# A two-block transformer kernel: order of work in the attention pairs and the convolution branch of the first block

## The reference

```
proj = u @ w_in                       # q, k, v, conv input a | g, gates g_attn | g_conv
attn = softmax(q k^T / 8, causal) v   # 8 heads of 64 (one key block of 256: plain causal attention)
h    = a * sigmoid(g)
h    = depthwise_conv(h, 31 taps) + b # 512 channels
h    = silu(layer_norm(h))
y    = (sigmoid(g_attn) * (attn @ w_attn_br) + sigmoid(g_conv) * (h @ w_conv_pw)) @ w_out
x    = layer_norm(alpha * x + (1 + gt1) * y)
x    = layer_norm(alpha * x + (1 + gt2) * (relu(u2 @ w_up)^2 @ w_down))
```

## Time and profile before

| what | value |
|---|---|
| median of 3 runs | 1812.81 us (1811.41 to 1814.45) |
| span of the profiled execution | 1813.6 us (no other time of it is given) |
| PE busy | 1755.5 us, 97% |
| DVE busy | 1275.5 us, 70% |
| ACT busy | 891.5 us, 49% |
| DMA | 346.29 MB, mean 191 GB/s |
| mean granted TensorE clock | 0.997 |

### The profile page before, as it was taken

The page is one execution under the profiler, slowest core; times in us unless marked ns, Lnnn a source line. Parts: engine busy times, 40 slices in busy tenths (PEclk is TensorE's granted clock), DMA queues, the critical chain, the costliest instruction groups (busy, mean ns, idle before and its releaser), DMA issues.

```text
span 1813.6 us, 26735 instructions
## 1 busy us (share of the span) xinstructions
PE 1755.5 (97%) x9254; PEld 1450.9 (80%) x9254; DVE 1275.5 (70%) x1973; ACT 891.5 (49%) x1530; POOL 57.3 (3%) x111
## 2 busy tenths in 40 slices
PE   8999999998999999998999999999999999999998
PEld 3776778996766779987998977788889989778886
DVE  5788887667788885568557987655555588865555
ACT  1456434443455444444556664544455667544443
POOL 0000010000000000002000000000000000000000
PEclk9999999999999999999999999999999999999999
DMA  8866568774866566663665444555646645345553
GB/s 300 267 213 218 162 216 301 253 230 133 264 220 209 185 210 209 209 190 110 210 215 156 131 142 141 174 185 184 190 153 200 215 131 160 117 155 182 184 186 126
DMA packets 216040, 346.29 MB, mean 191 GB/s; under 512 B 19611, under 2 KB 113353, under 8 KB 215673
## 3 DMA queue, kind: packets, MB, share of 16 engines
q1 hardware_dynamic: 213448, 338.89, 58.3%
q0 software_dynamic: 1632, 5.39, 1.0%
q10 hardware_dynamic: 850, 0.54, 0.1%
HBM read 343.69 MB, written 1.07 MB: 190 GB/s over the span
## 4 chain that ended last, share of the span: by engine, by line
issue 79%; PE 12%; DVE 4%; DVEq 1%; POOLq 1%; POOL 1%; ACT 0%; DMA 0%; SPq 0%; ACTq 0%
PE acc L150 2%; PE acc L148 2%; PE acc L149 2%; PE prod L223 1%; PE prod L225 1%; PE prod L224 1%; DVE w_lo L134 1%; DVEq L937 1%; PE prod L148 1%; DVE proj L938 1%; PE prod L150 1%; PE prod L149 1%; PE turn L262 0%; DVE x_res L938 0%; DVE x_res L936 0%
## 5 line engine op out<-in xcount | busy, mean ns | idle before, releaser
L134 DVE TENSOR_TENSOR w_lo<-w_raw,w_hi 128x1024 fp32r<-128x1024 f32 (+2 forms) x584 | 643.7, 1122 | 308.6 <-ACT w_hi L128 302.9
L128 ACT CAST w_hi<-w_raw 128x1024 fp32r<-128x1024 f32 (+2 forms) x584 | 557.9, 968 | 406.6 <-PE acc L150 186.3
L148 PE MATMUL prod<-w_hi,hT_hi 128*128 128x512 f32 (+2 forms) x880 | 319.8, 363 | 4.7 <-ACT proj_b L1949 3.6
L150 PE MATMUL prod<-w_hi,hT_lo 128*128 128x512 f32 (+2 forms) x880 | 313.0, 356 | 0.0
L149 PE MATMUL prod<-w_lo,hT_hi 128*128 128x512 f32 (+2 forms) x880 | 312.3, 355 | 0.0
L148 PEld LDWEIGHTS prod<-w_hi,hT_hi 128*128 128x128 f32 x880 | 166.3, 189 | 25.0 <-DVE gates L2202 5.9
L150 PEld LDWEIGHTS prod<-w_hi,hT_lo 128*128 128x128 f32 x880 | 166.3, 189 | 15.4
L149 PEld LDWEIGHTS prod<-w_lo,hT_hi 128*128 128x128 f32 x880 | 166.8, 189 | 14.6
L223 PE MATMUL prod<-uT_hi,w_hi 128*128 128x256 f32 x448 | 127.1, 284 | 1.6 <-DVE w_lo L134 1.1
L148 PE MATMUL prod<-w_hi,uT_hi 128*128 128x512 f32 x304 | 124.6, 410 | 2.7 <-DVE uT_lo L301 1.3
L224 PE MATMUL prod<-uT_lo,w_hi 128*128 128x256 f32 x448 | 126.4, 282 | 0.0
(11 more groups left out here) (349 smaller groups left out, 2836.6 us busy)
## 6 DMA issues: line engine op xcount, KB each, us to landing
w_raw<-in_w_in_dram SPq DMA_DIRECT2D x72, 512.0 KB, 3.8
ada_raw<-in_w_ada_dram SPq DMA_DIRECT2D x68, 512.0 KB, 6.7
w_raw<-in_w_in_dram SPq DMA_DIRECT2D x192, 172.0 KB, 2.4
w_raw<-in_w_up_dram SPq DMA_DIRECT2D x64, 512.0 KB, 4.4
w_raw<-in_w_down_dram SPq DMA_DIRECT2D x64, 512.0 KB, 4.5
w_raw<-in_w_gate_dram SPq DMA_DIRECT2D x128, 192.0 KB, 2.6
w_raw<-in_w_ffn_gate_dram SPq DMA_DIRECT2D x88, 256.0 KB, 3.6
w_raw<-in_w_ffn_up_dram SPq DMA_DIRECT2D x88, 256.0 KB, 4.3
```

Source lines behind the costliest of these rows:

```text
L128: act.copy(self.hi[:, s, 0:cols], self.raw[:, s, 0:cols]).then_inc(self.hi_done, 1)
L134: dve.tensor_tensor(self.lo[:, s, 0:cols], self.raw[:, s, 0:cols], self.hi[:, s, 0:cols].bitcast(F32), ALU.subtract).then_inc(self.lo_done, 1)
L148: pe.matmul(out, a_hi, w_hi, start=first and c == 0, stop=False)
L150: mm = pe.matmul(out, a_lo, w_hi, start=False, stop=last and c == chunks - 1)
```

## The change

On DVE the minima of the scores, in every pair, stand directly behind the gating, ahead of `steps(counts[1])`, and these steps follow behind the inverses together with `counts[2]`. On ACT, in the last pair alone, the order behind `split_hi(nxt + 2)` becomes: copies of the turned probabilities, tanh of the gate tile, partial sums, high part of the attention rows, copy of the modulation sum, `split_hi(nxt + 3)`, `conv_take`. On TensorE the last `mod_sum` moves from behind group `at + 1` to directly behind `pair_end(3)`, ahead of the wait for the attention rows' low part. Behind the pairs ACT makes two weight halves ahead of the tanh of the convolution's rows instead of three behind them, and two behind the takes of the convolution's rows instead of one. DVE makes one low half ahead of its takes of these rows instead of two. No instruction is added or left out.

```
@@ ACT, pair(t) @@
                     W.split_hi(act, nxt + 2)
-                    take_tile(nt, this + 3, [...], ACT.Tanh, 0.5)
-                    W.split_hi(act, nxt + 3)
+                    gate_take = lambda: take_tile(nt, this + 3, [...], ACT.Tanh, 0.5)
+                    if t < PAIRS - 1:
+                        gate_take()
+                        W.split_hi(act, nxt + 3)
                     for h in range(2):
                         H.take(act, n, h)
+                    if t == PAIRS - 1:
+                        gate_take()
                     part_take(2 + t)
                     H.out_hi_part(act, n, ...)
+                    if t == PAIRS - 1:
+                        ada_take(layer(l, 2 + t, SUMS), chunk(mod2, NT), acc[1:2])
+                        W.split_hi(act, nxt + 3)
                     conv_take(t, layer(l, F_TAPS[t], F_ALL))
                     if t < PAIRS - 2:
                         hpad_take(t + 2, l)
-                    ada_take(layer(l, 2 + t, SUMS), chunk(mod2, NT), acc[1:2])
+                    if t < PAIRS - 1:
+                        ada_take(layer(l, 2 + t, SUMS), chunk(mod2, NT), acc[1:2])
 
                 for t in range(PAIRS):
                     pair(t)
+                split(layer(l, G_IN + G_HALF, G1), 2)
                 for tok in range(TOKS):
                     act.wait_ge(conv_y, layer(l, tok, TOKS).count(1))
                     act.activation(conv_sig[:, tok, :], conv_tok[:, tok, :], ACT.Tanh, scale=0.5).then_inc(conv_tanh, 1)
-                split(layer(l, G_IN + G_HALF, G1), 3)
                 for n in range(2):
                     T.take_hi(act, layer(l, F_CONV + n, F_ALL), cT[0][:, :, n * P:(n + 1) * P], scale=0.5,
                               view=lambda s: s.rearrange("p (c t) -> p c t", c=4))
-                split(layer(l, G_IN + G_HALF + 3, G1), 1)
+                split(layer(l, G_IN + G_HALF + 2, G1), 2)
@@ DVE, pair(t) @@
                     if t < PAIRS - 2:
                         gated(t + 2)
-                    steps(counts[1])
                     for h in range(2):
                         H.lows(dve, n, h, None, None)
                     W.split_lo(dve, nxt + 1)
                     for h in range(2):
                         H.inverse(dve, n, h)
-                    steps(counts[2])
+                    steps(counts[1] + counts[2])
@@ DVE, behind the pairs, j is the half of the branch's columns @@
                     W.split_lo(dve, layer(l, at + 4 + 2 * j, G1))
-                    W.split_lo(dve, layer(l, at + 5 + 2 * j, G1))
+                    if j == 1:
+                        W.split_lo(dve, layer(l, at + 5 + 2 * j, G1))
                     if j == 0:
                         for n in range(2):
                             place = lambda p: p[:, :, n * P:(n + 1) * P]
                             T.take_lo(dve, layer(l, F_CONV + n, F_ALL), ...)
+                        W.split_lo(dve, layer(l, at + 5 + 2 * j, G1))
@@ TensorE @@
                 pair_end(PAIRS - 1)
+                mod_sum(1 + PAIRS, acc[1])
                 pe.wait_ge(H.out_done, layer(l, PAIRS - 1, PAIRS).count(2))
                 at = G_IN
                 W.multiply(pe, layer(l, at, G1), aT, 0, NT, KG, outs, True, False, vacant=...)
                 conv_turn(PAIRS - 1)
                 W.multiply(pe, layer(l, at + 1, G1), aT, 2, NT, KG, outs, False, True)
-                mod_sum(1 + PAIRS, acc[1])
```

More of the change, by code:

```diff
@@ L837, in pair @@
                     W.split_hi(act, nxt + 2)
-                    take_tile(nt, this + 3, [chunk(proj[:, tok, :], NT, GA0) for tok in range(TOKS)], ACT.Tanh, 0.5)
-                    W.split_hi(act, nxt + 3)
+                    gate_take = lambda: take_tile(nt, this + 3, [chunk(proj[:, tok, :], NT, GA0) for tok in range(TOKS)],
+                                                  ACT.Tanh, 0.5)
+                    if t < PAIRS - 1:
+                        gate_take()
+                        W.split_hi(act, nxt + 3)
                     for h in range(2):
                         H.take(act, n, h)
+                    if t == PAIRS - 1:
+                        gate_take()
                     part_take(2 + t)
                     H.out_hi_part(act, n, aT[0][:, t, :] if last else aT[0][:, bass.ds(t, 1), :].rearrange("p a s -> p (a s)"))
+                    if t == PAIRS - 1:
+                        ada_take(layer(l, 2 + t, SUMS), chunk(mod2, NT), acc[1:2])
+                        W.split_hi(act, nxt + 3)
                     conv_take(t, layer(l, F_TAPS[t], F_ALL))
```

## The result

| | before | after |
|---|---|---|
| median | 1812.48 us (4 runs, 1811.41 to 1814.45) | 1804.01 us (4 runs, 1800.67 to 1806.32) |
| ratio, 95% interval | | 0.9949 (0.9936 to 0.9962) |
| span of the profiled execution | 1813.6 us | 1798.9 us |
| from the end of pair 0's scores to the convolution branch's product, layer 0 | 84.82 us | 80.38 us |
| the same, layer 1 | 83.77 us | 80.28 us |

A forecast was written before the change was run, and what follows sets the result against it. TensorE, busy 97%, was taken as the bound, with time only in its gaps or slow-clock stretches. Layer 0's 1.98 + 0.73 and layer 1's 1.07 + 0.73 made 4.5 us: median 1808.3 us, range 1806.5 to 1811.3.

The forecast's parts named there:

- The lead as pair 3 begins: Pairs 1 and 2: transposes freed of waits for scaled probabilities, gaining 0.85 + 0.22 = 1.07 us.
- the first reading of the prediction: TensorE, whole program: waits for scaled probabilities cost 2.5 us in four places, the size of what the change can reach.
- Pair 3: Last pair: transposes gain another 0.56 us; the value product starts directly behind the modulation rows, at 178.65 instead of 181.46.
- The next bound: Convolution's turn: fourth w_hi holds DVE 1.4 us, TensorE waits 2.0; turn 1.98 us earlier in layer 0, 1.07 in layer 1.
- Behind the turn: Convolution's rows: takes ahead of weight halves remove the 0.65 us wait and 0.1 of semaphore, 0.73 us per layer.
- New wait of DVE for the scores: DVE, pairs 1 to 3: minima would wait for the scores themselves, estimated 0.5 us, less than DVE gained.
- Weight loads: Loads on SP: up to 2 us earlier or as before, priced at 0, bounded by 0.5 us of contention.
- The fall of the clock on the path: Group behind the second turn of rows: a clock fall costs 1.4 us in that layer, 1809.7; chance 0.15.
- (b): Convolution chain gives nothing: late fourth w_hi leaves the turn in place, only 0.73 us per layer remain, 1811.3; chance 0.12.
- (d): Slower: two clock falls in each layer, at the new idle and around the normalized rows, 1815.5; chance 0.03.
- (c): More than summed: vanishing clock fall gives layer 1 0.9 us, DVE held less by w_hi up to 1; 1806.5; chance 0.13.
- The rule that speaks against it: Activity releases the clock throttle, so the new 2.0 us idle before the convolution's turn is a likelier place for a fall.

The follow-up runs named there:

- w_hi ahead of the sum's copy: The change, with ScalarE making the fourth w_hi ahead of the copy of the modulation sum in the last pair; 1802.92 us, ratio 0.9946.
- sum back: The change, with the last modulation sum back behind the attention branch's second group and its copy on ScalarE back behind the pair; 1802.51 us, ratio 0.9942.
- steps earlier: The change, with three last-pair convolution steps moved into the projection, two ahead of the low part, fourth w_hi directly behind the gates; 1800.03 us, ratio 0.9928.
- second head later: The kernel before, with the second head's transposes behind the modulation rows in pairs 0 to 2; 1811.06 us, ratio 0.9991.
- minima only: The kernel before, with only DVE's minima moved ahead of the convolution steps, in every pair; 1805.38 us, ratio 0.9958.
- copy behind the tanh: The change, with the modulation sum back behind the second group and its ScalarE copy behind the two tanh of the convolution's rows; 1803.10 us, ratio 0.9953.
- minima in the last pair: The kernel before, with DVE's minima moved in the last pair alone; 1809.60 us, ratio 0.9989.
- the run without its minima: The whole change, with DVE's minima left where they were before; 1810.46 us, ratio 0.9996.
- the run without its tail: The whole change, with the order of weight halves behind the pairs as before, on ACT and DVE; 1805.98 us, ratio 0.9965.

## Why the prediction was wrong

The mechanism was right in nearly every place, and one term was too small. Layer 1 has no clock fall on either side, so the sum is held against it; leads are counted from pair 0's scores.

- *The lead as pair 3 begins.* Forecast 1.07 us (0.85 in pair 1, 0.22 in pair 2), measured 2.31 (the scores of pair 3, 572.26 to 562.05, less the 7.90 that pair 0's were early). **This is the step that failed.** The missing 1.24 (1.32 in layer 0) are three times 0.33 from the wait inside the row of six transposes, and 0.25 from the first transposes of pairs 0 to 2, which follow the last matmul by 0.23 us and not by the 0.32 that I estimated (pair 0 was not in the sum at all). The row was read as work of 1.15 us. It was 0.82 of work and 0.33 of waiting for ScalarE, which the weight loads show. With it falls the first reading of the prediction, that the 2.5 us of printed waits are the size of what the change can reach: the idles of DVE ahead of the third w_lo, 4.0 us per layer, were a better measure, and the prediction had named them (about 1 us per pair) without letting them into the sum.
- *Pair 3.* The first transposes gained 0.63 more (forecast 0.56), the second head's again 0.33 that were not in the sum. The value product follows the modulation rows, 2.60 us behind the first transpose, where I said 3.02.
- *The next bound.* As forecast: the fourth w_hi, behind the sum's copy, holds DVE, and the turn waits. Measured DVE idle 1.02 us (forecast 1.4), TensorE's wait 1.58 (2.0). The turn's gain was 2.67 us in layer 1 where I had 1.07, and 3.69 in layer 0 where I had 1.98; the differences, 1.60 and 1.71, are the lead's 1.24 and 1.32 and some 0.4 of pair 3.
- *Behind the turn.* Forecast 0.73 us per layer, measured 0.75 and 0.82; undone alone, 0.80. The move of the sum was forecast at no gain for TensorE, and that holds.
- *New wait of DVE for the scores.* Forecast 0.5 us in pairs 1 to 3. It did not come: TensorE, freed of more waits than I counted, reached the scores just as DVE did, and DVE idles at most 0.15 us there.
- *Weight loads.* Priced at 0, with a bound of 0.5 us that rests on no row. Inside the stretches the traces before and after show no wait of an engine for a load.
- *Rivals.* The fall of the clock on the path did not occur in the profiled execution, (b) and (d) neither. (c), more than I sum, pointed the right way, but of its two reasons only a part came (DVE held 1.02 us by w_hi instead of 1.4), the larger lead was not among them, and its 1806.5 was still too slow.
- *The rule that speaks against it.* The new idle of 1.58 us drew no fall. In the five profiled kernels whose sum stands ahead of the attention branch, none of ten layers has its group at half clock; in the six others it is five of twelve. The Trainium skill's sentence on activity (page "TensorE: Matmul & The Clock Gate", section "Part 1: The HAM clock gate") agrees with this as read for the place that the change made busier, and the prediction had read it only for the place that the change made idler. That the sum is the cause is not shown: among the runs that differ ahead of the group in nothing but the sum and its copy it is none of two layers with it (w_hi ahead of the sum's copy) against one of four without (the two runs with the sum back). The effect is worth 0.91 us in a layer where it occurs; the profiled execution before had it in one, and no trace shows how often the other executions have it.

Of the 7.9 us by which both stretches shrank, then: about 7.0 are order (3.5 in each layer) and 0.91 the clock in layer 0. The measured 8.5, by its interval 7 to 12, agrees with either figure, 7.0 or 7.9.

The two profiled spans differ by 14.7 us, 6.8 more than the stretches, and the traces say where. The first weight product begins 2.7 us earlier, 0.7 lies between the two stretches (a part that spreads by 1.0 us over the eleven profiled kernels), and 3.3 lies behind the stretch of layer 1: from there to the end it is 1213.4 us before and 1210.1 after. That last part goes with the clock in a region that no edit touches, between 866 and 887 us. It is 1210.1 and 1210.7 us in the two profiled kernels without a half-clock stretch there (the change and steps earlier), 1212.1 to 1212.9 in the four with one of some 3.4 us, and 1213.2 to 1214.7 in the five with some 6.8 us. The runs that share most of the change are spread over all three, so as far as these traces tell this is no gain of the change.

Not tried: a version of the kernel before with DVE freed and the hidden wait kept, which would weigh the two alone. The experiments show that the minima move brings the gain, that the wait was inside the row, and that taking it out in pairs 0 to 2 without freeing DVE brings nothing.

## What to carry to other kernels

A merged row of like instructions can hold a wait: compare its length with the same row where nothing waits (here 1.15 us against 0.82), or read the weight-load side. Where an engine off the critical path (here DVE) paces the one on it, an early release counts only by how much idle it takes out of the pacing engine; the waits of the paced one then fall by themselves, and cannot be had one by one. Before an instruction that waits is moved ahead, list what stands behind it in its queue: here a 0.6 us copy held a weight half, the turn and, in another order, two weight halves and the tanh.

## What was not expected of the hardware

- One microsecond of matmuls put into a wait went with a steady clock: half clock in the next group in 0 of 10 layers with it and in 5 of 12 without. Where the clock fell, the idle ahead of that group was 1.20 and 0.94 us (before, and second head later), 1.7 (minima only, and copy behind the tanh) or 1.8 (minima in the last pair); with the sum ahead it is 0.64 in the change and 1.1 in the run without its minima. In the run with the sum back the same 1.70 us of idle drew no fall in either layer, so idle of this size makes a fall possible, not certain.
- The idle of 1.58 us ahead of the turn, about 3 us later, drew none in the six layers of the change, the run without its tail and, shorter at 1.1, the run without its minima.
- The beginning of the first weight product wanders between 36.3 and 39.3 us over eleven profiled kernels that do not differ there. TensorE's first products double their speed at another moment: in the three kernels that begin at 39.2 to 39.3 it is near 23 us, in the others by 17.5 us. Of these seven begin at 36.3 to 36.8, and the eighth (sum back, 38.4) has one more stretch at granted clock 0.50, from 34.8 to 38.2. Its rows around that moment, before:

```profile
19.33 3.78 PE L1403 MATMUL acc<-w_spare,c_wide 128*128 128x512 f32 x4
...
24.09 1.98 PE L1403 MATMUL acc<-w_spare,c_wide 128*128 128x512 f32 x4
```

and after:

```profile
13.80 3.60 PE L1413 MATMUL acc<-w_spare,c_wide 128*128 128x512 f32 x4
...
18.38 1.98 PE L1413 MATMUL acc<-w_spare,c_wide 128*128 128x512 f32 x4
```

  This alone is up to 3 us of the spread of whole times, more than most of the single edits here are worth.
